# Gram products of two heads issued alternately on the two row halves of TensorE, and one product with the state for both heads

## The reference

```
S_t = S_{t-1} diag(w_t) + (S_{t-1} (-kk_t)) (kk_t * a_t)^T + v_t k_t^T
o_t = S_t r_t
```

## Time and profile before

| | |
|---|---|
| median of 3 runs | 1607.19 us |
| span of the profiled execution (first to last instruction) | 1601.0 us |
| what lies around the span, against the median | 6.2 us |
| TensorE busy (matmul) | 1399.6 us, 87% |
| VectorE / ScalarE / GpSimd busy | 906.4 / 724.2 / 605.4 us |
| mean granted TensorE clock | 0.931 of full speed |
| stretch of the eight pairs | about 1096 to 1329 us after the start |
| one step of the loop | 26.99 us (the first grams of two steps stand at 1152.61 and 1179.60 us in the chain of waits) |

### The profile page before, as it was taken

How to read it: one execution, slowest core, us unless ns; L and a number is a source line. 1 busy time by engine, 2 the same in 40 slices (tenths; PEclk the granted TensorE clock), 3 DMA queues, 4 the chain that set the end, 5 groups by cost and what they waited for, 6 DMA issues and landing times. The chain is left out here.

```text
span 1601.0 us, 20851 instructions
## 1 busy us (share of the span) xinstructions
PE 1399.6 (87%) x6912; PEld 1141.1 (71%) x6912; DVE 906.4 (57%) x1436; ACT 724.2 (45%) x1209; POOL 605.4 (38%) x324
## 2 busy tenths in 40 slices
PE   5989998897999999997499966648999998799996
PEld 4877876675677777675377754537999986678885
DVE  2373353336688888884408999985666655301102
ACT  4455464434666767565443314442322322434442
POOL 5857667240000000004487425503000005477784
PEclk9989997598999999999799987869999999899998
DMA  6646532044798989894564424502000004345562
GB/s 201 177 124 168 153 131 80 0 141 146 237 321 298 322 281 336 279 334 136 139 197 140 126 77 145 157 16 92 2 1 0 0 1 161 116 140 174 180 187 79
DMA packets 127254, 239.92 MB, mean 150 GB/s; under 512 B 16296, under 2 KB 32346, under 8 KB 127056
## 3 DMA queue, kind: packets, MB, share of 16 engines
q1 hardware_dynamic: 116384, 227.12, 44.5%
q10 hardware_dynamic: 10801, 11.89, 2.7%
HBM read 234.79 MB, written 1.05 MB: 147 GB/s over the span
## 5 line engine op out<-in xcount | busy, mean ns | idle before, releaser
L278 POOL TENSOR_TENSOR wlo<-raw,whi 128x1024 fp32r<-128x1024 f32 (+1 forms) x232 | 562.8, 2444 | 758.6 <-ACT whi L273 758.0
L273 ACT ACTIVATE whi<-raw 128x1024 fp32r<-128x1024 f32 (+1 forms) x364 | 375.5, 1053 | 294.2 <-PE bank L286 230.0
L284 PE MATMUL bank<-whi,t0h 128*128 128x512 f32 (+1 forms) x1072 | 441.1, 411 | 56.8 <-POOL wlo L278 39.0
L285 PE MATMUL bank<-wlo,t0h 128*128 128x512 f32 (+1 forms) x1072 | 428.0, 399 | 0.0
L286 PE MATMUL bank<-whi,t0l 128*128 128x512 f32 (+1 forms) x1072 | 427.5, 399 | 0.0
L284 PEld LDWEIGHTS bank<-whi,t0h 128*128 128x128 f32 x1072 | 206.9, 193 | 117.6 <-issue 56.7
L286 PEld LDWEIGHTS bank<-whi,t0l 128*128 128x128 f32 x1072 | 205.6, 192 | 48.4
L285 PEld LDWEIGHTS bank<-wlo,t0h 128*128 128x128 f32 x1072 | 206.1, 192 | 44.7 <-issue 1.7
L278 DVE TENSOR_TENSOR wlo<-raw,whi 128x1024 fp32r<-128x1024 f32 x132 | 157.1, 1221 | 24.8 <-ACT whi L273 23.4
L2027 DVE SCALAR_TENSOR_TENSOR work<-work,proj 128x256 f32<-128x256 f32 x210 | 133.8, 696 | 2.0
L356 PE MATMUL bank<-const,work 128*128 128x128 f32 x128 | 29.4, 423 | 66.3 <-DVE work L444 55.1
(11 more groups left out here) (410 smaller groups left out, 1993.4 us busy)
## 6 DMA issues: line engine op xcount, KB each, us to landing
raw<-in_w_ff SPq DMA_DIRECT2D x64, 512.0 KB, 3.5
raw<-in_w_exp_down SPq DMA_DIRECT2D x124, 256.0 KB, 4.6
raw<-in_w_in SPq DMA_DIRECT2D x60, 496.0 KB, 3.7
raw<-in_w_in SPq DMA_DIRECT2D x56, 512.0 KB, 3.6
raw<-in_w_exp_gate SPq DMA_DIRECT2D x66, 256.0 KB, 4.9
raw<-in_w_exp_up SPq DMA_DIRECT2D x66, 256.0 KB, 5.9
proj<-in_w_exp_gate SPq DMA_DIRECT2D x62, 256.0 KB, 4.4
proj<-in_w_exp_up SPq DMA_DIRECT2D x62, 256.0 KB, 5.4
```

The lines of the kernel that those rows point to most:

```text
L273: nc.scalar.activation(whi[:, s, 0:width], raw_of(n)[:, 0:width], ACT.Copy).then_inc(hi_ready, 1)
L278: ins = (nc.vector if split_by_vector(n) else nc.gpsimd).tensor_tensor(wlo[:, s, 0:width], raw_of(n)[:, 0:width], whi[:, s, 0:width].bitca ...
L284: nc.tensor.matmul(dst, hi, wh, start=first, stop=False)
L285: nc.tensor.matmul(dst, hi, wl, start=False, stop=False)
```

## The change

The units are renumbered, so that the two heads of one tile share a group. The gram products of both heads are issued alternately: head 0 on the array's rows 0 to 63 into bank 5, head 1 on rows 64 to 127 into bank 4. The second call waits for both masks of the first. In `rest` and `outputs` of tile 1 the product with the state `SB` is one product of 128 columns for both heads, in place of two of 64 columns.

```diff
         def unit(h, t):
-            return 2 * h + t
+            return 2 * t + h
...
                 pe.wait_ge(*ft_copied.at(2 * p + 2))
-                for u in units:
-                    h, t = u // 2, u % 2
-                    if u >= 2:
-                        pe.wait_ge(*gram_masked.at(4 * p + u - 1))
-                    r = slice(64 * h, 64 * h + 64)
-                    ar = AR[c][r, t].rearrange("p a s -> p (a s)")
-                    for j in range(2):
-                        mm = nc.tensor.matmul(bank[5 - u % 2][:, 256 * j:256 * j + 256], BK[r, j, t, :], ar,
+                t = units[0] // 2
+                if t:
+                    pe.wait_ge(*gram_masked.at(4 * p + 2))
+                for j in range(2):
+                    for h in range(2):
+                        r = slice(64 * h, 64 * h + 64)
+                        ar = AR[c][r, t].rearrange("p a s -> p (a s)")
+                        mm = nc.tensor.matmul(bank[5 - h][:, 256 * j:256 * j + 256], BK[r, j, t, :], ar,
                                               start=True, stop=True)
-                    mm.then_inc(gram_done.sem, 1)
+                        if j:
+                            mm.then_inc(gram_done.sem, 1)
...
                 if t:
                     pe.wait_ge(s_ready, p + 1)
+                    nc.tensor.matmul(bank[6][:, 0:P], AR[c][:, 1, 0, :], SB, start=True, stop=False)
                 for h in range(2):
                     f = slice(h * DH, (h + 1) * DH)
-                    if t:
-                        nc.tensor.matmul(bank[6][:, f], AR[c][:, 1, 0, :], SB[:, f], start=True, stop=False)
                     mm = nc.tensor.matmul(bank[6][:, f], gram[c][:, unit(h, t), 256:384],
-                                          rkv[:, t, ds(2 * D + P * p + DH * h, DH)], start=t == 0, stop=True)
+                                          rkv[:, t, ds(2 * D + P * p + DH * h, DH)], start=t == 0, stop=t == 0 or h == 1)
...
-                if t:
-                    nc.tensor.matmul(oh, AR[c][:, 1, 1, :], SB[:, f], start=True, stop=False)
+                if t and h == 0:
+                    nc.tensor.matmul(bank[7][:, P:2 * P], AR[c][:, 1, 1, :], SB, start=True, stop=False)
                 nc.tensor.matmul(oh, gram[c][:, unit(h, t), 128:256], Uo[:, t, f], start=t == 0, stop=False)
```

More of the change, by code:

```diff
@@ L2300, in outputs @@
                 oh = bank[7][:, t * P + h * DH:t * P + (h + 1) * DH]
-                if t:
-                    nc.tensor.matmul(oh, AR[c][:, 1, 1, :], SB[:, f], start=True, stop=False)
+                if t and h == 0:
+                    nc.tensor.matmul(bank[7][:, P:2 * P], AR[c][:, 1, 1, :], SB, start=True, stop=False)
                 nc.tensor.matmul(oh, gram[c][:, unit(h, t), 128:256], Uo[:, t, f], start=t == 0, stop=False)
                 mm = nc.tensor.matmul(oh, gram[c][:, unit(h, t), 384:512],
-                                      rkv[:, t, ds(2 * D + P * p + DH * h, DH)], start=False, stop=True)
+                                      rkv[:, t, ds(2 * D + P * p + DH * h, DH)], start=False, stop=t == 0 or h == 1)
                 if t == 1 and h == 1:
```

## The result

The change is faster: the ratio to the kernel before is 0.9932 (95% interval 0.9918 to 0.9946), that is 10.9 us of 1606.6, with 8.7 and 13.2 us at the ends of the interval; forecast were 11.7. The median went from 1606.6 to 1594.3 us, where the forecast was 1595.5. Single executions of either kernel differ by several us (1597.8 to 1608.7 before, 1591.5 to 1596.1 after), so the ratio says roughly how much, and the traces say where. The span of the profiled execution went from 1601.0 to 1592.2 us.

What follows compares the result with a forecast made beforehand. TensorE's instruction stream was taken to bound the loop until VectorE's masks are late. Terms 1.1 (pair 0) + 5.8 (six steps) + 1.2 (step 7) + 3.6 (state products) = 11.7 us, from 1607.2 to 1595.5; range 1591.5 to 1600.5.

Steps and rivals of the forecast that it cites:

- What bounds the kernel: In the pairs' loop, TensorE's instruction stream sets the step length, busy 26.98 of 27 us, until another engine is late.
- TensorE pieces only: From the grams on, the chain of waits in a step was said to consist of TensorE pieces alone.
- slack of 0.5 us: VectorE's second start of the inverse precedes its use in `below(0)` by 0.5 us, said to decide the change's worth.
- The gram call: Both row halves stream side by side, so a gram call takes 1.10 us instead of 1.92, saving 0.82.
- strict program order: Variant within the forecast: matmuls start in program order, a gram call takes 1.28 us, total some 0.4 us longer.
- VectorE takes over: In steps 0 to 5 VectorE's masks hold the second call and `decays`: 0.96 us gained instead of 1.64, 5.8 in all.
- the masks don't bind: Rival, chance 0.06: VectorE's chain has room, all gram calls gain 0.82 us, total 16.2 us, time 1591.0 us.
- Step 7 and the end: Step 7 has no `decays`; `solve` behind ScalarE's table load comes 1.2 us earlier; the stretch to the merge gains 2.1.
- Pair 0: At pair 0 the last parameter row's landing holds VectorE's first mask, so 1.1 us is gained instead of 1.64.
- The state products: In `rest` and `outputs`, two records of 128 columns replace four of 64: 0.445 us per pair, 3.6 us in all.
- The clock falls in the loop: Rival, chance 0.04: some 0.9 us of idle time a step lowers TensorE's clock; 10 us slower, 1617.
- no overlap: Rival, chance 0.07: gram calls keep 1.92 us, only the state products gain 3.6 us, time 1603.6 us.

Runs made afterwards that it cites:

- e1: Kernel before with only the state products merged for both heads, grams as before: step 26.54 us, ratio 0.9980 to the kernel before.
- e5: Kernel after with the products of `decays` in bank 5 instead of 4, waiting for the third gram mask, not the fourth: step 25.44 us against 25.66.
- e3: Kernel after with each gram call issuing both products of head 0, then both of head 1: step 25.65 us, ratio 0.9939 to the kernel before.
- e4: Kernel after with each VectorE gram mask on only the first 256 of 512 columns, results not the reference's: step 24.90 us.
- e6: Kernel after with VectorE's level-6 masks moved ahead of the first start of the inverse: step 25.53 us, 0.12 less.
- e9: Kernel after run once more, unchanged: step 25.65 us, ratio 0.9947 to the kernel before.
- e7: Kernel after with VectorE's wait for the parameter rows moved to before their first reader: pair 0 to pair 1 27.29 us against 28.11; ratio 0.9944.

## Why the prediction was right

- **What bounds the kernel**: right in the main. Everything taken from TensorE's stream in the levels of the inverse counted at once (e1). But "TensorE pieces only" overlooked one wait a step, of 0.21 us, for ScalarE's copy before `solve`. And the slack of 0.5 us at the second start of the inverse is not what decides: in e5 `below(0)` waits for that start, and the step gets shorter all the same. What decides is when the fourth mask lets `decays` go, since `solve` follows it at 1.63 us. The forecast came out right because its own sum went by `decays` too.
- **The gram call**: forecast 1.10 us, measured 1.06. The lag between halves is 0.01 us, not 0.04. The strict program order, for which I had priced 1.28 us a call and 0.4 us in all, is out (the call itself, and e3).
- **VectorE takes over**: right in mechanism and place. Forecast 0.96 us a step, measured 0.89; e4 gives the rest back when the masks are made shorter, so the rival "the masks don't bind" is out. The missing 0.07 lies in one term, the start of `decays`: I put 0.04 us between the end of the mask and the next weight load, which holds for the second gram call (0.05) but not here: the fourth mask ends at 1183.39 and the load starts at 1183.54, 0.15 later (0.15 in e6 too). The trace has a register instruction of L2200 (it computes an address from the pair's number) between that wait and the load. `grow`, which also came late (0.12 us behind its mask), has one too, and the second gram call has none; that they are the cause is argued from this and was not tried.
- **Step 7 and the end**: forecast 1.2 and 0.9, 2.1 together; 2.41 measured, of which 0.4 is the luck of a trace without low clock. In step 7 `solve` starts 7.03 us behind the pair's grams in place of 8.13: 1.1 us and not 1.2, since `grow` is late as above. With the state products that makes 2.0, as against e3 and e9.
- **Pair 0**: the late parameter row was forecast as the limit and e7 shows it. The term was 0.3 us too good: I took the landing of the trace before, 3.6 us, and it was 4.0. In the twelve traces it is anything from 3.4 to 4.0 us, so this term carries some 0.3 us of chance either way.
- **The state products**: 3.6 us forecast, 0.45 a step measured, eight times that is 3.6.
- **The clock falls in the loop**: it stayed at 1.00 in every step of every trace, with idle time of about half a microsecond in it, where the rival counted 0.9. Out, as is "no overlap".
- **The range**, 1591.5 to 1600.5, held. That the median, 1594.3, lies 1.2 us below the forecast is the spread of the executions, since by the two traces less was gained, 10.9 us and not 11.7: pair 0, the six steps and step 7 fell short by 0.3, 0.5 and 0.1, what follows took 0.3 more, and the clock gave 0.4 back. What makes single executions differ by several us is not in the terms of the sum: in the ten traces after the first one, pair 0's grams start anywhere from 1091.7 to 1104.2 us, while a step of the loop repeats to 0.02 us from trace to trace (after and e9).

## What to carry to other kernels

When TensorE's work in a stage is made shorter, lay the consumer's instructions end to end first: here VectorE's masks had about 0.5 us of slack ahead of `decays`, and about half of the gain in the grams arrives. Then follow what hangs on the late instruction through the other engines: here `decays` counts because ScalarE serves it before the copy that `solve` waits for. Ask of each new wait whether it is for data or only for a bank, since another bank can make it shorter (e5). For products on 64 rows, put both row halves into one call, into different banks, without a wait between them; in the two orders tried, the order in the program made no difference (e3).

## What the runs showed of the hardware

- Float32 products on the two row halves, into different banks, run side by side at no loss: head 0's fourth record starts 0.75 us after its first with and without the other half beside it, and head 1's records 0.01 us behind head 0's, in both orders of the program (after and e3). The halves behave like two queues. Both halves into one bank were not tried.
- VectorE's masks of 512 float32 columns last 0.69 us and follow each other at 0.60; those of 256 last 0.42 and follow at 0.33.
- Beside GpSimd's split of a weight, VectorE's instruction on 256 columns that reads SBUF only (L2575) takes 1.49 us in place of 0.42 (1.22 in the kernel before), while the masks, which read PSUM, keep their 1.29 us for two. Timeline of the kernel after, at pair 0:

```profile
1099.91 1.29 DVE L2566 TENSOR_TENSOR work<-bank,const 128x512 f32<-128x512 f32 x2 [5.74 <-PE bank L2228]
1100.04 2.40 POOL L278 TENSOR_TENSOR wlo<-raw,whi 128x1024 fp32r<-128x1024 f32 x1 [0.40 <-ACT whi L273]
1101.23 1.49 DVE L2575 SCALAR_TENSOR_TENSOR work<-work,const 128x256 f32<-128x256 f32 x1
```

  GpSimd's instruction ends at 1102.44 and VectorE's at 1102.72, 0.28 us later. It is 0.28 in all 24 places of the twelve traces, whether VectorE's instruction started 0.94 us or 1.74 us before that end. So it looks as if it got on only when GpSimd's was done. No run took the GpSimd work away, so this is read from the timelines alone.
